# The seams between phases of a two-block transformer kernel, done token block by token block

## The chip, the cores and the metric

One core of a Trainium2 chip runs the whole program. The metric is device time in microseconds, the median of several runs; a profiled execution shows where it goes.

## What is computed

256 tokens of width 2048 go through two transformer blocks, all in float32. What matters here is the chain of matrix products and the norms between them:

```python
# first block (attention left out)
x = x + rmsnorm(mix @ w_out, post_mix_g)
h = rmsnorm(x, pre_ffn_g)
u = causal_dwconv(h @ w_up, conv_w, conv_b)
gate, val = split(u)
y = (gelu(gate) * val) @ w_down          # 5632 -> 2048
x = x + rmsnorm(y, post_ffn_g)
# second block
h = rms_norm(x, norm_attn_w) * (1 + sc_a) + sh_a
q, k, v, u = split(h @ w_in)
x = x + g_a * (concat(attn, pool) @ w_out)
hm = rms_norm(x, norm_mlp_w) * (1 + sc_m) + sh_m
x = x + g_m * (square(relu(hm @ w_up)) @ w_down)   # 2048 -> 8192 -> 2048
return rms_norm(x, final_norm_w)
```

A norm runs along the 2048 columns of a token, so it needs the last column chunk of the product before it, but only for that token.

## The kernel before

The 256 tokens are two blocks of 128 (`b` = 0, 1), one token per partition. Every product goes through column chunks of 512. A chunk is accumulated over the depth in steps of two 128-row tiles: 8 steps for a depth of 2048, 6 in the third down phase ("down1c"). Phases follow one another in the table `PHASES`; those of interest end with down1c and are followed by in2 (seam A), out2 followed by mlp2 (seam B), and the end of mlp2 (the tail, C).

Precision comes from a split of each number into a rounded high part and the rest, so each product is three matmuls: high by high, high by low, low by high. For a step's weights (512 KB) SyncE loads a slot of `raw` (8 slots, `load`, L347), ScalarE writes the high part `w_hi` (`hi`, L573), VectorE the rest `w_lo` (`lo`, L1047), each 128 x 1024, into a ring of 4 slots. `hi(s)` waits for the weights in `raw` and, through `step_done`, for step s-4 to be done; `lo(s)` waits for `hi(s)`; `load` of step s+8 waits for `lo(s)`. TensorE's `step` (L1755) waits for both and runs 12 matmuls, both blocks together, six each. Into PSUM tensor `G` go the products, two banks for an even chunk and two for an odd one; `T` takes transposes.

The activations of a new phase are made from `x`: rows are scaled by the reciprocal norm into `y` (`scale_rows`, block 0 on ScalarE and block 1 on VectorE, or both on VectorE for mlp2), TensorE transposes them (`turn`, L1789, eight units of 256 columns, four transposes of 128 x 128 each), ScalarE applies gain and shift in two 256-wide activations and copies to `h_hi` (`high_shifted`, L559), VectorE subtracts for `h_lo` (`low_shifted`, L1130). Semaphores count the units: `xn_act`, `xn_dve`, `prep_turned`, `prep_hi`, `h_ready`.

Each engine's program is written out by hand and runs strictly in order; a `begin` on each engine (ScalarE, VectorE, TensorE) interleaves the eight units with the first steps. In the last chunk, `last_steps` (L1818) does only the last two steps block by block, so block 0 ends 12 matmuls earlier. Then VectorE sums and weighs it (L1527 on for seam A, L1654 on for B, L1700 on for C), ScalarE squares it, `root` makes one reciprocal norm for both blocks, and only then does `begin` start. In seam A the norm needs two roots: that of y, and that of the new x, got from sums of squares and cross products (`cross`, L1455; L1540 on) before the new x exists. `down_body` (ScalarE L832, VectorE L1459) puts the norm of the context rows (`ctx_squares`, `root("ctx")`, `ctx_scale`) and the squares of finished y chunks between the weight splits of the down1c chunks.

At the end of the kernel the output is scaled and stored in four transfers of 512 KB, two per block, when the norm of both blocks is known.

Of the kernel before, what the change touches and what calls it, by code (L numbers as in the profile page):

```python
# [69 lines left out]
STEPS = 2 * LOADS  # L70
UP0 = {"up1a": 0, "up1b": 8, "up1c": 16, "mlp2": 22}
# [34 lines left out]
def build(nc, a):  # L106
# [83 lines left out]
    dup1 = place("dup1", [P, NB, 2, 2, DH], "x")  # L190
    dup2 = place("dup2", [P, 2 * NB, KV2, 2, DH], "tmp")
# [321 lines left out]
    def _(act):  # L513
# [58 lines left out]

        def hi(s, d=0, width=N):  # L573

            act.wait_ge(raw_full[s % 8], 32 * (s // 8 + 1) + d * 4)
            if s >= 4:
                act.wait_ge(step_done, s - 3 + d)
            act.activation(w_hi[:, s % 4, :, 0:width], raw[:, s % 8, :, 0:width],  # L578
                           ACT.Copy).then_inc(hi_ready, 1)
# [252 lines left out]
        def down_body(s, c):  # L832

            if c == 1:
                his(s + 3, 3)
                y_squares(0)
                his(s + 6, 3)
            elif c == 2:
                act.wait_ge(ctx_in, 16)
                hi(s + 3)  # L840
                ctx_squares(0)
                hi(s + 4)
                ctx_squares(1)
                hi(s + 5)
                y_squares(1)
                hi(s + 6)
                ctx_squares(2)
                hi(s + 7)
                ctx_squares(3)
                hi(s + 8)  # L850
            else:
                hi(s + 3)
                root("ctx")
                hi(s + 4)
# [38 lines left out]
        act.wait_ge(bank_evac, FIRST_EVAC["in2"] - 1)  # L893
        square(y[:, 0, 3 * N:4 * N], sq[:, 0, 3:4])
        act.wait_ge(crossed, 4)
        square(u_buf[:, 0, :], dots[:, 0, 0, 3:4])
        act.wait_ge(bank_evac, FIRST_EVAC["in2"])
        square(y[:, 1, 3 * N:4 * N], sq[:, 1, 3:4])
        act.wait_ge(crossed, 5)
        square(u_buf[:, 1, :], dots[:, 0, 1, 3:4])  # L900
        root("y2")
        root("in2")
        scale = scale_rows(x, y, lambda q: rstdx[:, 0:1])
        act.wait_ge(rstd_ready, STAT["in2"] + 1)

        def in2_scale(q):
            act.wait_ge(x_new, X_NEW["in2"] + q + 1)
            scale(q)

        begin(2 * FIRST_LOAD["in2"], lambda q: high_shifted("in2", q, comb, adac[:, 0, :], h_hi), in2_scale)  # L910


# [71 lines left out]
        for c in range(4):  # L984
            if c == 0:
                his(s0 + 7, 4)
            else:
                if c == 3:
                    sqrt_table()
                body(s0 + 8 * c, n=7 if c == 3 else 8)  # L990
                new_squares("out2")(c - 1)
        for b in range(NB):
            act.wait_ge(x_new, X_NEW["out2"] + 3 + b + 1)
            square(x[:, b, 3 * N:4 * N], sq[:, b, 3:4])
        root("up2")
        begin(2 * FIRST_LOAD["mlp2"], lambda q: high_shifted("up2", q, comb, adac[:, 3, :], h_hi))
# [1256 lines left out]
```

## Time and profile before

| | us |
|---|---|
| median of 3 runs | 2223.4 |
| lowest and highest | 2220.48, 2223.8 |
| profiled execution, its own time | 2221.93 |
| its span, first to last instruction | 2220.2 |
| mean granted TensorE clock | 0.982 |

The page gives busy times by engine, the chain of work that ended last and the costliest groups. Questions to the trace give a timeline (start, duration, engine, line, operation, count, idle time before it and what ended it), groups by line with mean durations, and sums by stretch. PE is TensorE, ACT is ScalarE, DVE is VectorE, SPq is SyncE's DMA queue. A granted clock of 1 is 2.4 GHz, 0.5 is 1.2 GHz. Times in a timeline count from the start of the span.

### The profile page before, as it was taken

The numbers are of one execution on the slowest core, as the hardware profiler recorded it, in microseconds if no ns is written. First come the engines' busy times: TensorE is split into PE (matmuls) and PEld (weight loads), VectorE is DVE, ScalarE is ACT, GpSimd is POOL, SyncE is SP. The second block draws the span as 40 slices with busy tenths as digits, with TensorE's granted clock in tenths as the row PEclk, the third lists the DMA queues.
The fourth block names the chain that finished last, engine by engine and source line by source line (L and its number), as shares of the span: only waits on it lengthen the run. The fifth ranks groups of instructions, "written<-read, shape, count | busy, mean of one in ns | idle before, by whom it ended". The sixth has DMA issues, their size and how long they took to land.

```text
span 2220.2 us, 32332 instructions
## 1 busy us (share of the span) xinstructions
PE 2170.0 (98%) x10240; PEld 1796.3 (81%) x10240; DVE 1509.0 (68%) x1884; ACT 1078.0 (49%) x1449; POOL 133.5 (6%) x233
## 2 busy tenths in 40 slices
PE   8999999999999999999989999999999999999998
PEld 7888887888788888888867778878888887888876
DVE  7996788788896887767675354556545655655656
ACT  6545655555334554355477355454434433433433
POOL 3110001000110000100000000000000000000000
PEclk9999999999999999999989999999999999999999
DMA  9887087888896888978745341547666665766652
GB/s 338 294 261 234 2 301 226 263 278 268 264 300 222 263 276 282 321 221 256 228 133 182 99 158 48 173 159 268 212 194 228 223 195 183 244 191 210 226 173 103
DMA packets 277677, 482.85 MB, mean 217 GB/s; under 512 B 25996, under 2 KB 118484, under 8 KB 276256
## 3 DMA queue, kind: packets, MB, share of 16 engines
q1 hardware_dynamic: 247168, 367.22, 50.5%
q0 software_dynamic: 30192, 113.72, 16.7%
q8 instruction: 83, 1.36, 0.2%
q14 instruction: 58, 0.48, 0.1%
q10 hardware_dynamic: 176, 0.08, 0.0%
HBM read 478.81 MB, written 2.11 MB: 217 GB/s over the span
## 4 chain that ended last, share of the span: by engine, by line
PE 94%; ACT 2%; DVE 2%; issue 1%; DMA 0%; POOL 0%; ACTq 0%; DVEq 0%; POOLq 0%
PE G L1769 28%; PE G L1771 28%; PE G L1770 28%; PE T L2035 1%; PE T L2149 1%; PE T L1842 1%; PE T L1956 1%; PE T L1800 1%; PE G L1936 1%; PE G L2129 1%; ACT w_hi L578 1%; ACT junk L524 0%; PE T L1981 0%; DVE w_lo L1052 0%; PE T L1983 0%
## 5 line engine op out<-in xcount | busy, mean ns | idle before, releaser
L1052 DVE TENSOR_TENSOR w_lo<-raw,w_hi 128x1024 fp32r<-128x1024 f32 x696 | 839.5, 1217 | 462.1 <-ACT w_hi L578 459.7
L578 ACT ACTIVATE w_hi<-raw 128x1024 fp32r<-128x1024 f32 x696 | 732.3, 1055 | 849.8 <-PE G L1771 844.1
L1769 PE MATMUL G<-w_hi,h_hi 128*128 128x512 f32 (+1 forms) x1904 | 749.9, 394 | 7.9 <-issue 4.2
L1771 PE MATMUL G<-w_hi,h_lo 128*128 128x512 f32 (+1 forms) x1904 | 742.1, 390 | 0.0
L1770 PE MATMUL G<-w_lo,h_hi 128*128 128x512 f32 (+1 forms) x1904 | 741.8, 390 | 0.0
L1769 PEld LDWEIGHTS G<-w_hi,h_hi 128*128 128x128 f32 x1904 | 360.1, 189 | 82.5 <-issue 7.8
L1771 PEld LDWEIGHTS G<-w_hi,h_lo 128*128 128x128 f32 x1904 | 359.8, 189 | 74.8
L1770 PEld LDWEIGHTS G<-w_lo,h_hi 128*128 128x128 f32 x1904 | 360.4, 189 | 71.6
L1769 PE MATMUL G<-w_hi,a_hi 128*128 128x512 f32 x880 | 347.4, 395 | 2.2 <-issue 1.1
L1771 PE MATMUL G<-w_hi,a_lo 128*128 128x512 f32 x880 | 345.1, 392 | 0.0
L1770 PE MATMUL G<-w_lo,a_hi 128*128 128x512 f32 x880 | 345.0, 392 | 0.0
L1769 PEld LDWEIGHTS G<-w_hi,a_hi 128*128 128x128 f32 x880 | 167.0, 190 | 39.2 <-issue 3.5
L1770 PEld LDWEIGHTS G<-w_lo,a_hi 128*128 128x128 f32 x880 | 166.9, 190 | 35.0 <-issue 0.5
L1771 PEld LDWEIGHTS G<-w_hi,a_lo 128*128 128x128 f32 x880 | 166.7, 189 | 35.1
L446 POOL DMA_DIRECT2D ada_w<-in_w_ada x192 | 101.9, 531 | 1419.8 <-DVE ada_acc L1070 894.9
L1070 DVE SCALAR_TENSOR_TENSOR ada_acc<-ada_w,silu,ada_acc 128x1024 f32<-128x1024 f32 x122 | 153.7, 1280 | 30.5 <-DMA ada_w<-in_w_ada 30.4
L1070 DVE SCALAR_TENSOR_TENSOR ada_third<-ada_w,silu,ada_third 128x1024 f32<-128x1024 f32 x60 | 76.9, 1282 | 57.8 <-DMA ada_w<-in_w_ada 57.8
L1160 DVE SCALAR_TENSOR_TENSOR ada_acc<-ada_w,silu,ada_acc 128x1024 f32<-128x1024 f32 x64 | 79.2, 1279 | 0.2 <-DMA ada_w<-in_w_ada 0.2
L1417 DVE SCALAR_TENSOR_TENSOR conv<-T,convw,conv 128x255 f32<-128x255 f32 (+1 forms) x176 | 72.6, 475 | 7.0 <-ACT conv L809 4.7
L601 ACT ACTIVATE u_buf<-G,rstdx 128x512 f32<-128x512 f32 x44 | 27.9, 686 | 34.8 <-PE G L1771 34.5
L815 ACT ACTIVATE conv<-conv 128x512 f32<-128x512 f32 x22 | 13.9, 633 | 60.6 <-DVE conv L1417 60.6
L809 ACT ACTIVATE conv<-T,convw 128x256 f32<-128x256 f32 x88 | 42.5, 563 | 0.8
(273 smaller groups left out, 1225.9 us busy)
## 6 DMA issues: line engine op xcount, KB each, us to landing
ada_w<-in_w_ada POOLq DMA_DIRECT2D x192, 512.0 KB, 5.0
raw<-in_w_up SPq DMA_DIRECT2D x352, 256.0 KB, 4.5
raw<-in_w_mlp_up SPq DMA_DIRECT2D x256, 256.0 KB, 2.9
raw<-in_w_mlp_down SPq DMA_DIRECT2D x256, 256.0 KB, 3.4
raw<-in_w_in SPq DMA_DIRECT2D x208, 256.0 KB, 4.0
raw<-in_w_down SPq DMA_DIRECT2D x176, 256.0 KB, 4.8
raw<-in_w_out SPq DMA_DIRECT2D x128, 256.0 KB, 3.8
raw<-in_w_in SPq DMA_DIRECT2D x16, 136.0 KB, 3.5
```

The source lines that it names most:

```text
L446: pool.dma_start(ada_tiles(run)[:, half, :], w_ada[:, bass.ds(t + first // 2, 1), part * D + half * ADA_HALF:part * D + (half + 1) * ADA_HALF]
L578: act.activation(w_hi[:, s % 4, :, 0:width], raw[:, s % 8, :, 0:width], ACT.Copy).then_inc(hi_ready, 1)
L601: act.activation(dst(b), G[:, 2 * parity + b, 0:width], func, scale=scale).then_inc(bank_evac, 1)
L809: ins = act.activation(conv[:, j, :], tt(0)[:, j, :], ACT.Identity, scale=convw[:, 2, bass.ds(t + dt, 1)], bias=convw[:, 3, bass.ds(t + dt ...
L1052: dve.tensor_tensor(w_lo[:, s % 4, :, 0:width], raw[:, s % 8, :, 0:width], w_hi[:, s % 4, :, 0:width].bitcast(F32), ALU.subtract).then_inc ...
L1070: ins = dve.scalar_tensor_tensor(out=acc[:, half, :], in0=ada_tiles(run)[:, half, :], scalar=silu[:, c, bass.ds(dt + (first + k) // 2, 1)] ...
L1160: ins = dve.scalar_tensor_tensor(out=ada_acc[:, c, half, :], in0=ada_w[:, half, :], scalar=silu[:, c, k // 2:k // 2 + 1], in1=ada_acc[:, c ...
L1417: ins = dve.scalar_tensor_tensor(out=conv[:, j, k:TOK], in0=tt(0)[:, j, 0:TOK - k], scalar=convw[:, tap, bass.ds(t + dt, 1)], in1=conv[:, ...
L1769: pe.matmul(out, ah, wh, start=f, stop=False)
L1770: pe.matmul(out, ah, wl, start=False, stop=False)
L1771: mm = pe.matmul(out, al, wh, start=False, stop=l)
L1800: mm = pe.transpose(bank(q)[:, TOK * j + b * P:TOK * j + b * P + P], src[:, b, (2 * q + j) * P:(2 * q + j + 1) * P], ident)
```

## The change

- The last chunk of down1c, out2 and mlp2 runs all its steps for block 0 and then all for block 1 (`last_chunk`). For that, all its weights must stand at once, so SBUF regions that are free then take some steps' halves (`SLOT`, `halves`): two at seam A, four at B, four in the tail. `hi` waits for the last user of its own slot (`BEFORE`).
- Each norm at these places is made per block: roots `y2_0`, `in2_0`, `y2_1`, `in2_1`, `up2_0`, `up2_1`, `final_0`, `final_1`.
- Activations of in2 and mlp2 are made in eight parts of one block and 512 columns (`PARTS`), in place of units of both blocks and 256 columns. `high_part` uses four 128-wide activations and one copy; `in2_scale` is 512 wide. At seam A ScalarE scales the parts of block 0, at seam B VectorE scales all.
- The first chunk of in2 and mlp2 runs steps 0 to 5 for block 0, then for block 1, then steps 6 and 7 for both (`first_chunk`); transposes of the parts stand between. The first two parts (A) or three (B) are turned inside the last chunk's block-1 pass.
- In down1c the context norm moves one chunk earlier in `down_body`. ScalarE's chunk 1 is now `his(s+3, 3)`, `y_squares(0)`, then `hi` of s+6, s+7, s+8 with `ctx_squares(0)` and `(1)` between; its chunk 2 is `hi(s+3)`, `ctx_squares(2)`, `hi(s+4)`, `ctx_squares(3)`, `hi(s+5)`, `y_squares(1)`, `root("ctx")`, `hi(s+6)`, four `ctx_scale`, `hi(s+7)`, four `ctx_scale`, `hi(s+8)`; its chunk 3 is `his(s+3, 3)`, `y_squares(2)`. VectorE's root, scaling and cross products follow suit. `cross` of the last chunk writes its unused product to PSUM.
- At the end each block is normed, scaled and stored by itself.

The diff, cut to its core; first the tables and ScalarE:

```diff
+IN2, OUT2, UP2 = (2 * FIRST_LOAD[n] for n in ("in2", "out2", "mlp2"))
+SLOT = {s: s % 4 for s in range(STEPS)}
+SLOT |= {IN2 - 6 + k: ("in2", k) for k in range(2)} | {IN2 + 4 + k: ("in2", k) for k in range(2)}
+SLOT |= {UP2 - 8 + k: ("act", k) for k in range(4)} | {UP2 + 4 + k: ("act", k) for k in range(2)}
+SLOT |= {STEPS - 8 + k: ("h", k) for k in range(4)}
+PARTS = ((0, 0), (0, 1), (0, 2), (1, 0), (1, 1), (1, 2), (0, 3), (1, 3))
...
+        def high_part(name, u, gain, shift):
+            act.wait_ge(prep_turned, PREP[name] + u + 1)
+            if u >= 2:
+                act.wait_ge(h_ready, PREP[name] + u - 1)
+            for j in range(4):
+                k = 4 * PARTS[u][1] + j
+                ins = act.activation(split_part(u)[:, j, :], bank(u)[:, P * j:P * j + P], ACT.Identity,
+                                     scale=gain[:, k:k + 1], bias=shift[:, k:k + 1])
+            ins.then_inc(tmp_act, 1)
+            act.wait_ge(tmp_act, SHIFTED[name] + u + 1)
+            act.activation(part_of(h_hi, u), split_part(u), ACT.Copy).then_inc(prep_hi, 1)
...
-            if s >= 4:
-                act.wait_ge(step_done, s - 3 + d)
+            if BEFORE[s] is not None:
+                act.wait_ge(step_done, BEFORE[s] + 1 + d)
...
+        y2_squares(0)
+        root("y2_0", 0, 1)
+        hi(IN2)
+        root("in2_0", 0, 1)
+        act.wait_ge(rstd_ready, STAT["in2_0"] + 1)
+        in2_scale(0)
+        in2_scale(1)
+        in2_high(0)
+        hi(IN2 + 1)
+        in2_scale(2)
+        y2_squares(1)
+        in2_high(1)
+        hi(IN2 + 2)
+        root("y2_1", 1, 1)
+        in2_high(2)
+        root("in2_1", 1, 1)
+        his(IN2 + 3, 2)
+        in2_high(3)
+        hi(IN2 + 5)
+        in2_scale(6)
+        in2_high(4)
+        in2_high(5)
+        in2_high(6)
+        hi(IN2 + 6)
+        in2_high(7)
+        hi(IN2 + 7)
...
+        x_square("out2", 0)
+        root("up2_0", 0, 1)
+        up2_high(0)
+        hi(UP2)
+        up2_high(1)
+        hi(UP2 + 1)
+        up2_high(2)
+        hi(UP2 + 2)
+        x_square("out2", 1)
+        root("up2_1", 1, 1)
+        hi(UP2 + 3)
+        hi(UP2 + 4)
+        up2_high(3)
+        hi(UP2 + 5)
+        up2_high(4)
```

On VectorE, again for seam A and then for seam B:

```diff
+        y2_sum(0)
+        y2_cross(0)
+        y2_root(0)
+        in2_root(0)
+        in2_rows(0)
+        lo(IN2)
+        in2_rows(1)
+        in2_low(0)
+        lo(IN2 + 1)
+        in2_rows(2)
+        y2_sum(1)
+        in2_low(1)
+        lo(IN2 + 2)
+        y2_cross(1)
+        y2_root(1, lambda: in2_low(2))
+        in2_root(1, lambda: lo(IN2 + 3))
+        in2_rows(3)
+        lo(IN2 + 4)
+        in2_rows(4)
+        in2_low(3)
+        lo(IN2 + 5)
...
+        x_sum(0)
+        root("up2_0", rstdx[:, 0:1], blocks=slice(0, 1))
+        scale_part(0)
+        scale_part(1)
+        scale_part(2)
+        up2_low(0)
+        lo(UP2)
+        up2_low(1)
+        lo(UP2 + 1)
+        up2_low(2)
+        lo(UP2 + 2)
+        x_sum(1)
+        root("up2_1", rstdx[:, 1:2], at=1, blocks=slice(1, 2), meanwhile=lambda: lo(UP2 + 3))
+        scale_part(3)
+        scale_part(4)
+        lo(UP2 + 4)
+        scale_part(5)
+        up2_low(3)
+        lo(UP2 + 5)
```

On TensorE:

```diff
+        def last_chunk(s, n, acts, e, ready, between=lambda k: None):
+            pe.wait_ge(bank_evac, e)
+            block_steps(s, range(n), 0, 1, acts, n - 1, ready)
+            block_steps(s, range(n), 1, 1, acts, n - 1, None, between)
...
+        def first_chunk(name, s, turned):
+            def part(b):
+                return lambda k: (h_ready, PREP[name] + PARTS.index((b, k // 2)) + 1)
+            def blocks(b, ks, *parts):
+                block_steps(s, ks, b, 0, H[0], 7, part(b))
+                for u in parts:
+                    turn_part(name, u)
+            blocks(0, (0, 1), *((2,) if turned < 3 else ()))
+            blocks(0, (2, 3))
+            blocks(0, (4,), 3)
+            blocks(0, (5,), 4, 5)
+            blocks(1, (0, 1), 6)
+            blocks(1, (2, 3), 7)
+            blocks(1, (4, 5))
+            steps(s, 6, 8, 0, H, lambda k: (h_ready, PREP[name] + UNITS))
```

`block_steps` runs six matmuls per step for one block, waits for `hi` and `lo` of a step in the block-0 pass only, and counts `step_done` in the block-1 pass only. On VectorE `y2_sum` adds the chunk's product to y and weighs it, `y2_cross` makes the cross product, `in2_rows` updates x for one part (and scales it, for block 1), `in2_low` subtracts for `h_lo`; `x_sum` is the like for seam B.

## Rows read from the trace of the kernel before

**Rows 1.** Page, busy time of each engine; and shares of the chain that ended last:
```profile
PE 2170.0 (98%) x10240; PEld 1796.3 (81%) x10240; DVE 1509.0 (68%) x1884; ACT 1078.0 (49%) x1449; POOL 133.5 (6%) x233
...
PE 94%; ACT 2%; DVE 2%; issue 1%; DMA 0%; POOL 0%; ACTq 0%; DVEq 0%; POOLq 0%
```

**Rows 2.** Stretches table: busy time, clock, DMA share, GB/s:
```profile
1147.50:1187.80 40.30, 29.89 (x130) 24.05 (x130) 32.24 (x60) 28.12 (x51) 0.00 (x0) 0.83 0.37 117
1473.80:1508.10 34.30, 29.66 (x129) 24.42 (x129) 24.87 (x40) 22.36 (x36) 6.12 (x6) 0.85 0.50 173
2209.40:2220.20 10.80, 0.00 (x0) 0.00 (x0) 4.24 (x10) 3.48 (x7) 0.00 (x0) 0.71 0.49 194
```

**Rows 3.** Timeline, TensorE, seam A: start, us, line, operation, count, idle before:
```profile
1147.20 0.39 PE L1833 MATMUL G<-w_hi,a_lo 128*128 128x512 f32 x1
1156.83 2.19 PE L1800 MATMUL T<-consts,y 128*128 128x128 f32 x8 [9.24 <-ACT y L545]
...
1160.85 0.78 PE L1769 MATMUL G<-w_hi,h_hi 128*128 128x512 f32 x1
...
1187.52 0.39 PE L1771 MATMUL G<-w_hi,h_lo 128*128 128x512 f32 x1
```

**Rows 4.** Timeline, TensorE, seam B:
```profile
1473.60 0.39 PE L1833 MATMUL G<-w_hi,h_lo 128*128 128x512 f32 x1
1477.73 2.82 PE L1800 MATMUL T<-consts,y 128*128 128x128 f32 x12 [3.75 <-DVE y L1113]
...
1507.25 0.39 PE L1771 MATMUL G<-w_hi,h_lo 128*128 128x512 f32 x1
...
1507.93 0.39 PE L1771 MATMUL G<-w_hi,h_lo 128*128 128x512 f32 x1
```

**Rows 5.** Timeline, TensorE, two other idle pieces:
```profile
367.38 2.82 PE L1800 MATMUL T<-consts,x 128*128 128x128 f32 x12 [2.83 <-DVE x L1363]
...
401.73 1.09 PE L2035 MATMUL T<-consts,u_buf 128*128 128x128 f32 x8 [1.36 <-ACT u_buf L601]
```

**Rows 6.** Groups by form, ScalarE: line, shapes, count, busy us, mean ns:
```profile
L578 ACT ACTIVATE w_hi<-raw 128x1024 fp32r<-128x1024 f32 x688 | 727.1, 1060 | 843.0 <-PE G L1771 837.3 <-DMA raw<-in_w_in 5.1
...
L567 ACT ACTIVATE conv<-T,adac,comb 128x256 f32<-128x256 f32 x32 | 16.1, 554 | 6.0 <-PE T L1800 5.9
...
L700 ACT ACTIVATE sm<-sm,nm 128x128 f32<-128x128 f32 x32 | 12.6, 394 | 24.0 <-DVE nm L1285 23.8
...
L692 ACT ACTIVATE vx<-p 128x128 f32<-128x128 f32 x2 | 0.5, 296 | 0.0
```

**Rows 7.** Timeline, ScalarE, seam A:
```profile
1149.16 0.63 ACT L524 ACTIVATE junk<-y 128x512 f32<-128x512 f32 x1 [2.64 <-DVE y L1532]
1149.69 0.18 ACT L524 ACTIVATION_READ_ACCUMULATOR junk<-y 128x1 f32 x1
...
1159.01 0.63 ACT L571 ACTIVATE h_hi<-conv 128x512 fp32r<-128x512 f32 x1
```

**Rows 8.** Groups by form, VectorE:
```profile
L1052 DVE TENSOR_TENSOR w_lo<-raw,w_hi 128x1024 fp32r<-128x1024 f32 x688 | 833.9, 1223 | 458.3 <-ACT w_hi L578 456.1 <-DVE ones_again L1092 0.2
L1070 DVE SCALAR_TENSOR_TENSOR ada_acc<-ada_w,silu,ada_acc 128x1024 f32<-128x1024 f32 x122 | 153.7, 1280 | 30.5 <-DMA ada_w<-in_w_ada 30.4
...
L1363 DVE SCALAR_TENSOR_TENSOR x<-y,rstd,x 128x256 f32<-128x256 f32 x28 | 12.1, 480 | 0.1
```

**Rows 9.** Timeline, VectorE, around seam B and at the end:
```profile
1454.73 1.22 DVE L1052 TENSOR_TENSOR w_lo<-raw,w_hi 128x1024 fp32r<-128x1024 f32 x1
...
2192.61 3.49 DVE L1052 TENSOR_TENSOR w_lo<-raw,w_hi 128x1024 fp32r<-128x1024 f32 x3
...
2209.39 0.69 DVE L1336 TENSOR_TENSOR y<-G,row 128x512 f32<-128x512 f32 x1 [0.50 <-PE G L1833]
...
2212.23 0.17 DVE L1105 RECIPROCAL rstdx<-ssq 128x2 f32<-128x2 f32 x1 [0.27 <-ACT ssq L535]
```

**Rows 10.** DMA query, 2212 to 2221 us: GB/s in 40 slices:
```profile
GB/s 0 0 0 0 0 0 0 0 0 309 419 419 419 400 364 419 437 400 400 382 401 437 400 364 419 419 383 437 364 437 437 364 91 0 0 0 0 0 0 0
```

More of the change, by code:

```diff
@@ L891, in _, with y2_squares, in2_scale, in2_high @@
                     body(s0 + per * c, n=per)
[L893 to L910, printed above, removed]
+        def y2_squares(b):
+            act.wait_ge(bank_evac, FIRST_EVAC["in2"] - 1 + b)
+            square(y[:, b, 3 * N:4 * N], sq[:, b, 3:4])
+            act.wait_ge(crossed, 4 + b)
+            square(u_buf[:, b, :], dots[:, 0, b, 3:4])
+        def in2_scale(u):
+            cols = slice(PARTS[u][1] * N, PARTS[u][1] * N + N)
+            act.wait_ge(x_new, X_NEW["in2"] + u + 1)
+            act.activation(y[:, 0, cols], x[:, 0, cols], ACT.Copy, scale=rstdx[:, 0:1]).then_inc(xn_act, 1)
+        def in2_high(u):
+            high_part("in2", u, comb, adac[:, 0, :])
+        y2_squares(0)
[24 more added lines that the diff above has]
+        hi(IN2 + 7)
         s0 = 2 * FIRST_LOAD["in2"]
@@ L1026, in _ @@
         for b in range(NB):
-            act.wait_ge(x_new, X_NEW["final"] + 3 + b + 1)
-            square(x[:, b, 3 * N:4 * N], sq[:, b, 3:4])
-        root("final")
-        act.wait_ge(rstd_ready, STAT["final"] + 1)
-        for b in range(NB):
+            x_square("final", b)
+            root(f"final_{b}", b, 1)
+            act.wait_ge(rstd_ready, STAT[f"final_{b}"] + 1)
             for c in (1, 3):
@@ L1525, in _, with y2_sum @@
                     ada_finish(fin_down)
-        for b in range(NB):
+        def y2_sum(b):
             if b == 0:
@@ L1558, in _ @@
+        lo(IN2 + 5)
+        in2_rows(5)
+        in2_rows(6)
+        in2_low(4)
+        in2_low(5)
+        in2_rows(7)
+        in2_low(6)
+        lo(IN2 + 6)
+        in2_low(7)
+        lo(IN2 + 7)
         cos = tab2[:, COS2:COS2 + 2 * DH].rearrange("p (b d) -> p b d", b=NB)
@@ L1837, in last_steps, with block_steps @@
                     mm.then_inc(block_done, 1)
+        def block_steps(s, ks, b, parity, acts, last, ready=None, between=lambda k: None):
+            hi, lo = acts
+            for k in ks:
+                if b == 0:
+                    pe.wait_ge(hi_ready, s + k + 1)
+                    pe.wait_ge(lo_ready, s + k + 1)
+                if ready is not None:
+                    pe.wait_ge(*ready(k))
+                whole, rest = halves(s + k)
+                for j in range(STEPK):
+                    ah, al = (t[:, STEPK * k + j, b * P:b * P + P] for t in (hi, lo))
+                    out = G[:, 2 * parity + b, :]
+                    pe.matmul(out, ah, whole[:, j, :], start=k == 0 and j == 0, stop=False)
+                    pe.matmul(out, ah, rest[:, j, :], start=False, stop=False)
+                    mm = pe.matmul(out, al, whole[:, j, :], start=False, stop=k == last and j == STEPK - 1)
+                if b == 1:
+                    mm.then_inc(step_done, 1)
+                elif k == last:
+                    mm.then_inc(block_done, 1)
+                between(k)
```

270 lines of the change are left out of this document (168 added, 102 removed).

## The prediction

> **What bounds the kernel now.** I read the page first: TensorE is busy 98% of the span and holds 94% of the chain that ended last [rows 1]. So only what makes TensorE's stream denser can shorten the kernel, and what delays it lengthens the kernel one for one. The stretches table shows the places of the edit [rows 2]. At the full clock a 512-wide matmul follows the one before by 0.227 us (three in 0.68) [rows 4], and four transposes take 0.43 (eight need 1.09, less the last one's own delay) [rows 5]. A first chunk is 96 matmuls and eight groups of four transposes, 21.8 + 3.4 = 25.2 us. Seam A (down1c to in2) takes 40.3, so 15.1 are lost: 9.24 idle in one piece while the norm is made [rows 3], and the rest to the clock, whose mean is 0.83, which makes 0.34 x 40.3 = 13.7 us at 1.2 GHz. Seam B (out2 to mlp2) takes 34.3 and loses 9.1, 3.75 of it one gap, mean clock 0.85 [rows 2, 4]. The tail C is 10.8 us behind the last matmul. The change can win at most about 15 + 9 + a few.
>
> **How I cost it.** All new orders are written out by hand, so I laid them on a timetable: an instruction starts when its engine is free and its last input has landed, plus 0.04 to 0.06 us. Laid over the old order from the last matmul of each phase, this ends seam A at 1187.9 and seam B at 1508.1; the trace has 1187.75 and 1508.16 [rows 3, 4], so the method is good to a few tenths. Prices: `hi` 1.06, `lo` 1.22, of which 0.08 to 0.1 overlaps the next instruction [rows 6, 8]; a square with its accumulator read 0.72 and an `h_hi` copy of 512 columns 0.63 [rows 7]; a two-tensor VectorE op over 512 columns 0.69, tiny ones 0.17 to 0.2 [rows 9]; a three-operand op over 512 columns 0.75, between 0.48 for 256 and 1.28 for 1024 [rows 8].
>
> **One new price.** `high_part` does a part as four 128-wide activations in place of two of 256. The 256-wide one takes 0.55, that is 1.02 for a unit's two [rows 6]. No row has it 128 wide: below it stand a plain 128-wide copy, 0.30, and a 128-wide exponential with a pointer bias, 0.39; above it the 256-wide 0.55 [rows 6]. I take 0.45 and 1.56 for four with overlap, ends 1.2 and 1.95. With the copy a part costs ScalarE 2.1 where a unit cost 1.55: eight parts make 4.4 us more on ScalarE per seam. (The Trainium skill, "ScalarE: Activation LUTs", section "What ACT_TABLE_LOAD costs", gives a fixed cost per activation, more with each pointer operand, and about 0.09 us of overlap; by its figures four would cost an estimated 1.64. The trace agrees at 256 columns.)
>
> **Seam A, the last chunk.** It must start at 1147.4 - 6 x 2.72 = 1131.1. Its block-0 pass wants a step's weights every 1.36 us. Context squares, root and scaling are moved into chunk 2, ahead of `hi(IN2-6)` to `hi(IN2-4)` on both engines, and the eviction of chunk 2 stands before `lo(IN2-3)`. My timetable has `lo(-4)` ready at 1134.6 and `lo(-3)` at 1136.9: TensorE waits 0.75 and 1.0. Block 0 ends at 1141.2 and block 1 would end at 1149.2. DVE is free at 1141.8 (chunk 2's cross products are queued ahead), the sum, norm and second root give the reciprocal for block 0 at 1146.7, `hi(IN2)` having slipped in between. Scaled columns come at 1148.2 and 1150.1, transposes of part 0 at 1148.8. So far this is as meant.
>
> **Seam A, the first chunk.** Here the new order ties the engines into a serial chain. Part 0 is split at 1153.0 (TensorE idle 2.5). `lo(IN2+1)` is ready at 1154.4, and only behind it and `in2_rows(2)` does VectorE take block 1's sum (1155.1). ScalarE has `y2_squares(1)` queued ahead of `in2_high(1)`, so part 1, whose transposes were done at 1150.7, waits until 1157.3, is low at 1160.3, and `lo(IN2+2)`, queued behind it, comes at 1161.8: TensorE idle 5.5. Then cross, root, `high(2)`, the second root, and only then `hi(IN2+3)`; `lo(IN2+3)` lands at 1169.6: idle 6.5. `lo(IN2+4)` at 1172.1: idle 1.2. Part 3's transposes stand on TensorE behind step 4; its split precedes `hi(IN2+5)`, `lo(IN2+5)` at 1178.6: idle 4.7. The last parts are ScalarE's 2.1 each, back to back, and the last `h_ready` comes at 1191.4. The chunk ends at 1196.9 at the full clock, 9.2 later than before. The order gives `hi` and `lo` of steps 2, 3 and 5 the place behind work that waits for block 1 or for TensorE; in the old order both engines kept running.
>
> **Seam B** by the same walk: the last chunk runs unbroken (eight weights in four spare slots; the old eviction of chunk 2 ended before 1454.9, `lo(UP2-5)` just in time), the norm of block 0 ends at 1466.3 and parts 0 to 2 are turned inside block 1's pass. The old gap of 3.75 goes, and the first chunk starts at 1475.2 rather than 1481.4. But `x_sum(1)` stands behind `lo(UP2+2)`, and square and root ahead of `hi(UP2+3)`: waits of 1.7, 3.7, 0.8 and 4.7 for `lo` of steps 2 to 5. End 1511.3, 3.2 later than before.
>
> **The tail C.** Before the last chunk VectorE evicts chunk 2 and gates it; its next `lo` start at 2192.6 [rows 9]. The chunk starts at 2187.4, its fourth step in single-block time at 2191.5, and needs the first of these, ready at 2193.9: 2.4 us lost. Behind the last matmul the chain of sum, square, root is as long as it was, 3.0 (2209.4 to 2212.4) [rows 9], but two of four output transfers have gone. The four ran 5.3 us at about 410 GB/s [rows 10], so two are worth 2.6, less the second's wait for its issue. Net -0.3, between -2.9 (no stall) and +1.
>
> **The clock.** After 3.75 us of idleness the transposes ran slow, twelve in 2.82 [rows 4], also after 2.83 [rows 5]; after 1.36 eight took 1.09 [rows 5]. The new gaps of 5.5, 6.5 and 4.7 in A and 3.7 and 4.7 in B are of the first kind. At 1.2 GHz from about 1160 to 1185 in A, the matmuls on the chain (three short bursts and transposes) double: A ends 3.4 later, +12.6, or +11 if it recovers in between; B gets +5 to +7. (The Trainium skill, "TensorE: Matmul & The Clock Gate", section "HAM oscillation — how this bites in real kernels", says that gaps in the matmul stream drop the clock again and again; rows agree for single gaps, none shows a run of them.)
>
> **Sum.** A +11, B +5.5, C -0.3: +16, on the profiled run's own 2221.9 (span 2220.2) 2238; it stands 1.5 under the median of 2223.4, on which the forecast is 2239.5. What follows either seam stays bound by TensorE and moves with it.
>
> **Rivals.** (1) Same order, clock stays at 2.4 GHz in most of it: A +9.2, B +3.2, C -0.3 = +12, 2235.5. For it: its pieces of work are short. Chance 0.25. (2) The clock stays low to the end of both first chunks and the block-0 passes starve more, because both engines must bring a step in 1.36 us where `lo` alone takes 1.14: A +15, B +8, C +1 = +24, 2247. Chance 0.13. The change would then not do what it says, finish block 0 early. (3) Faster: the norm of block 1 is in fact hidden. It decides at part 1: were its low half ready by the end of step 1 of block 0, 1155.8 (mine is 1160.3), and `lo` of steps 2 to 5 not late either, TensorE would idle in A only 1.75 + 0.5 + 2.5, keep its clock and lose 4.7 in place of 15.1; B would lose about 2 in place of 9.1; with C -0.3 that is -18, 2206. (The Trainium skill, "Perfetto Trace Analysis", section "Optimizing Scalar/DVE Operations", says that breaking up instructions can let work finish sooner where ScalarE or VectorE cause bubbles; by that rule it is this case.) Against it: the squares stand ahead of `in2_high(1)` in a queue that runs in order. Chance 0.08. (4) The stalls of A are half of mine and B comes out even or better: within 4 us. Chance 0.05.
>
> **Chances.** Forecast (A +10 to +13, B +4 to +7) 0.49, rivals 0.25, 0.13, 0.08, 0.05. About 0.2%, 4.4 us, is what a measurement here can tell. Slower 0.87, same 0.05, faster 0.08. The range takes in the low end of (1), with cheap 128-wide activations (A another 2 less) and no stall in C, 2228, and (2) in part: 2228 to 2249.
>
> **What would show it.** In A the profile after should show TensorE idle in four or five pieces of 2 to 7 us between 1150 and 1185, released by VectorE's `w_lo` and `h_lo`, a first chunk ending near 1197 to 1200, and ScalarE's squares of block 1 ahead of part 1's activations. In B matmuls start about 6 us earlier, yet the chunk ends later. In C TensorE waits once for `w_lo`. It would be wrong if the waits for `w_lo` of steps 2, 3 and 5 are short, or if part 1's activations run before block 1's squares.

## The result

The changed kernel takes 2239.5 us (median of 5 runs, 2230.7 to 2243.8) beside 2223.4 for the kernel before on the same chip (5 runs, 2214.5 to 2227.7): a ratio of 1.007, interval 1.0047 to 1.0092. Measured again, beside experiment 4, it gave 1.0083 (1.0058 to 1.0108). The sign and the size were as forecast; that the median met 2239.5 to a tenth is luck, since the interval is 10 us wide. The profiled execution is the shortest of the five; its own time is 2230.7, its span 2229.0. The page of after, which answers to [rows 1]:

```profile
span 2229.0 us, 32345 instructions
...
PE 2167.0 (97%) x10240; PEld 1790.1 (80%) x10240; DVE 1506.8 (68%) x1876; ACT 1084.0 (49%) x1481; POOL 133.0 (6%) x233
...
PE 94%; ACT 3%; issue 1%; DVE 1%; DMA 0%; POOL 0%; ACTq 0%; DVEq 0%; POOLq 0%
```

The page says little: TensorE still holds 94% of the chain. The stretches say more. Each runs from the start of the last chunk of a phase to the end of the next phase's first chunk (the third to the end of the span). Columns: stretch, length, busy time (count) by engine, granted clock, DMA share, GB/s. First the kernel before, which shows the whole seams where [rows 2] shows only their second parts, then after:

```profile
core 0 of [0], span 2220.2 us
...
1131.11:1187.75 56.64, 46.23 (x201) 37.33 (x200) 44.71 (x83) 40.62 (x75) 0.00 (x0) 0.88 0.43 135
1452.07:1508.16 56.09, 51.45 (x226) 42.27 (x224) 37.52 (x54) 33.20 (x51) 6.12 (x6) 0.91 0.55 181
2187.43:2220.20 32.77, 21.92 (x97) 17.83 (x95) 19.51 (x25) 10.85 (x18) 0.00 (x0) 0.90 0.16 65
```

```profile
core 0 of [0], span 2229.0 us
...
1126.00:1192.64 66.64, 47.91 (x202) 37.02 (x200) 43.22 (x71) 41.34 (x82) 0.00 (x0) 0.90 0.36 114
1456.94:1519.84 62.90, 53.40 (x226) 42.77 (x225) 32.86 (x46) 31.69 (x62) 5.04 (x4) 0.89 0.43 138
2196.35:2229.00 32.65, 22.21 (x97) 17.75 (x95) 19.87 (x28) 7.03 (x15) 0.00 (x0) 0.94 0.16 65
```

A is 10.0 longer, B 6.8, the tail 0.1 shorter: +16.7, where the forecast had +11, +5.5, -0.3, which makes +16.2. In the second trace of the same kernel (beside experiment 4) A is 66.9 and B 63.0 long. Where the 10 us of A are is seen in TensorE's waits. These rows answer to [rows 3]; the single wait of 9.24 is gone. In its place (start, duration, line, operation, count, idle before):

```profile
1129.51 0.47 PE L2036 MATMUL G<-w_hi,a_hi 128*128 128x512 f32 x1 [0.62 <-ACT w_hi L626]
...
1131.84 0.47 PE L2036 MATMUL G<-w_hi,a_hi 128*128 128x512 f32 x1 [0.72 <-issue]
...
1148.18 0.47 PE L2036 MATMUL G<-w_hi,h_hi 128*128 128x512 f32 x1 [2.29 <-ACT w_hi L626]
...
1156.76 0.61 PE L2036 MATMUL G<-w_hi,h_hi 128*128 128x512 f32 x1 [5.13 <-DVE w_lo L1147]
...
1164.23 0.77 PE L2036 MATMUL G<-w_hi,h_hi 128*128 128x512 f32 x1 [4.73 <-ACT in_hi L626]
...
1173.55 0.47 PE L2036 MATMUL G<-in_hi,h_hi 128*128 128x512 f32 x1 [4.51 <-issue]
```

The first two are the starved block-0 pass of down1c's last chunk, the next four stand before steps 0, 2, 3 and 5 of block 0. The names of the releasers mislead here. TensorE waits for `hi_ready`, `lo_ready` and `h_ready` together. At 1164.23 the page names ScalarE's `in_hi`, but VectorE's low half of step 3 ended at that moment: its row starts at 1162.91 and lasts 1.23. At 1173.55, "issue", a low half starts at 1172.22 and lasts 1.23. Why VectorE was late with them:

```profile
1157.36 0.16 DVE L1196 TENSOR_REDUCE ssq<-sq 128x1 f32<-128x4 f32 x1
1157.56 0.15 DVE L1197 TENSOR_SCALAR ssq<-ssq 128x1 f32<-128x1 f32 x1
1160.04 0.69 DVE L1229 TENSOR_TENSOR h_lo<-conv,h_hi 128x512 fp32r<-128x512 f32 x1 [2.33 <-ACT h_hi L619]
...
1162.91 1.23 DVE L1147 TENSOR_TENSOR w_lo<-raw,w_hi 128x1024 fp32r<-128x1024 f32 x1 [1.22 <-ACT w_hi L626]
```

VectorE is not busy, it stands in its own queue: idle 2.33 for part 2's high half, then 1.22 for `hi(IN2+3)`, which stands on ScalarE behind two roots and a part. Seam B shows the same kind of wait, 1.38, 3.27 and 4.51 before steps 2, 3 and 5, where [rows 4] had one of 3.75. The tail has the forecast stall:

```profile
2202.85 0.47 PE L2036 MATMUL G<-spare_hi,a_hi 128*128 128x512 f32 x1 [2.26 <-issue]
```

The profiled after is 8.8 longer in span, not 16.7, so it won 7.9 elsewhere: 5.1 ahead of A (which starts at 1126.0 here and at 1131.1 in before), nothing between A and B, 2.8 between B and the tail. Experiments 1 and 8 below take that up.

### The profile page after: what moved, and what is told of

Read it like the earlier page. It is cut to its first block, busy times and chain, and to the rows that moved or that the text cites. A ratio compares the mean times of both kernels' runs of the same rounds, so it can differ in the third digit from the quotient of the medians.

```text
span 2229.0 us, 32345 instructions
## 1 busy us (share of the span) xinstructions
PE 2167.0 (97%) x10240; PEld 1790.1 (80%) x10240; DVE 1506.8 (68%) x1876; ACT 1084.0 (49%) x1481; POOL 133.0 (6%) x233
## 3 DMA queue, kind: packets, MB, share of 16 engines
q1 hardware_dynamic: 247168, 367.22, 50.2%
q0 software_dynamic: 30192, 113.72, 16.7%
## 4 chain that ended last, share of the span: by engine, by line
PE 94%; ACT 3%; issue 1%; DVE 1%; DMA 0%; POOL 0%; ACTq 0%; DVEq 0%; POOLq 0%
PE G L1953 27%; PE G L1955 27%; PE G L1954 27%; PE T L2281 1%; PE T L2395 1%; PE G L2036 1%; PE T L2202 1%; PE G L2038 1%; PE G L2037 1%; PE T L2088 1%; ACT conv L615 1%; PE G L2182 1%; PE G L2375 1%; ACT w_hi L626 1%; PE T L1984 0%
## 5 line engine op out<-in xcount | busy, mean ns | idle before, releaser
L626 ACT ACTIVATE w_hi<-raw 128x1024 fp32r<-128x1024 f32 x682 | 716.5, 1055 | 813.5 <-PE G L1955 806.9
L1147 DVE TENSOR_TENSOR w_lo<-raw,w_hi 128x1024 fp32r<-128x1024 f32 x682 | 821.7, 1216 | 429.5 <-ACT w_hi L626 427.2
L1953 PE MATMUL G<-w_hi,h_hi 128*128 128x512 f32 (+1 forms) x1832 | 718.1, 392 | 6.2 <-issue 2.6
L1955 PE MATMUL G<-w_hi,h_lo 128*128 128x512 f32 (+1 forms) x1832 | 711.4, 388 | 0.0
L1954 PE MATMUL G<-w_lo,h_hi 128*128 128x512 f32 (+1 forms) x1832 | 710.9, 388 | 0.0
L1953 PEld LDWEIGHTS G<-w_hi,h_hi 128*128 128x128 f32 x1832 | 344.9, 188 | 78.0 <-issue 6.8
L1954 PEld LDWEIGHTS G<-w_lo,h_hi 128*128 128x128 f32 x1832 | 345.0, 188 | 68.5
L1953 PE MATMUL G<-w_hi,a_hi 128*128 128x512 f32 x840 | 331.2, 394 | 2.5 <-issue 1.7
L1954 PE MATMUL G<-w_lo,a_hi 128*128 128x512 f32 x840 | 329.0, 392 | 0.0
L1955 PE MATMUL G<-w_hi,a_lo 128*128 128x512 f32 x840 | 329.0, 392 | 0.0
```

Source lines behind the costliest of these rows:

```text
L626: act.activation(halves(s)[0][:, :, 0:width], raw[:, s % 8, :, 0:width], ACT.Copy).then_inc(hi_ready, 1)
L1147: dve.tensor_tensor(rest[:, :, 0:width], raw[:, s % 8, :, 0:width], whole[:, :, 0:width].bitcast(F32), ALU.subtract).then_inc(lo_ready, 1)
L1953: pe.matmul(out, ah, wh, start=f, stop=False)
L1954: pe.matmul(out, ah, wl, start=False, stop=False)
L1955: mm = pe.matmul(out, al, wh, start=False, stop=l)
```

## The experiments

My theory: the order of ScalarE's and VectorE's queues in the two first chunks makes a serial chain, and that is the loss. The rivals: TensorE's half clock; the extra ScalarE work of 128-wide activations; a loss that isn't in the seams at all. Lengths of A and B are always measured as above (56.6 and 56.1 in before, 66.6 and 62.9 in after).

**1. One part of the change at a time.** Three kernels, each the kernel before with one place changed.

```diff
 # A alone (PE; ScalarE's and VectorE's parts of the same seam go with it)
-        begin("in2", y, s0, 0, r)
-        steps(s0, 3, 8, 0, H, r)
+        first_chunk("in2", s0, 2)
 # B alone
-        begin("up2", y, s0, 0, r)
-        group2(s0, e0, u0, begun=3)
+        first_chunk("up2", s0, 3)
+        group2(s0, e0, u0, begun=8)
 # C alone
+                if last and c == 3:
+                    last_chunk(s + 56, 8, A[0], e + 12, ready)
```

> Of the change only seam A (down1c to in2) is made: context work moved into chunk 2, block-first last chunk, norm per block, first chunk by blocks. Seam B and the tail are those of before. Theory (the order of the two queues makes a serial chain in the first chunk): the trace of after has A 10.0 us longer than before, so 2223.4 + 10 = 2233.4, ratio 1.0045. Rival (the parts share the loss through the clock, what is won or lost elsewhere): if the 8 us that the profiled run won outside the seams belonged to the change, A alone would give about +5 or less, ratio under 1.0025.

> Of the change only seam B (out2 to mlp2) is made. Theory: the trace of after has B 6.8 us longer, so 2230.2, ratio 1.003; at the full clock my timetable gives +3.2, 1.0014, so a value between the two says how much the half clock adds. Rival (B is about even and the whole loss is A's): ratio 1.000.

> Of the change only the tail is made (last chunk by blocks in four spare slots, root per block, two of four output transfers early). Theory: 2.3 us of waiting for one low half and 2.6 us less of output transfer cancel: -0.1 to -0.3 us, ratio 0.9999. Rival (the stall costs more than the transfers give, or the other way round): off by over 2 us, ratio under 0.999 or over 1.001.

A alone: 1.0046 (1.0027 to 1.0064), its seam 66.9 long. B alone: 1.0027 (1.0011 to 1.0042), its seam 63.2. C alone: 0.9996 (0.9979 to 1.0013), with the same stall of 2.26. 1.0046 and 1.0027 are 10.2 and 6.0 us, and the seams are 10.3 and 7.1 longer than before's. So the loss lies in A and B, about 3 to 2, and the tail is even, as the walk (the prediction's timetable) had it.

**2. One swap at the point that the prediction named.** The prediction let its rival (3) decide at part 1, where ScalarE has block 1's squares ahead of `in2_high(1)`.

```diff
-        y2_squares(1)
         in2_high(1)
+        y2_squares(1)
         hi(IN2 + 2)
```

> The kernel after with one edit: on ScalarE in2_high(1) stands ahead of y2_squares(1), so that part 1 is split before block 1's squares. My prediction named this place as the point from which the other sign decides. Rival (that place alone makes the wait): the 5.1 us wait before step 2 of block 0 goes down by the two squares and more, about 3 us, and the time to about 3 us under after, ratio 1.0055 or less. Theory (both queues are tied together, so that one swap is not enough): VectorE has block 1's sum ahead of part 1's low half and the low half of step 2 behind it, and hi(IN2+2) still stands behind the squares; my timetable moves the wait by 0.1 us: ratio that of after, 1.007, and the wait before step 2 at 5.0 us.

Ratio 1.0076 (1.0052 to 1.01). The wait before step 2:

```profile
1159.76 0.77 PE L2036 MATMUL G<-w_hi,h_hi 128*128 128x512 f32 x1 [5.01 <-DVE w_lo L1147]
```

5.01 in place of 5.13: the timetable's 0.1, and nothing won. Part 1 was split 1.5 us earlier, but the squares now stood before `hi(IN2+2)`, so the low half of step 2 came no sooner. I had named the place rightly and its weight wrongly: it is one link of two that are late together. The other links were not swapped one by one.

**3. The order of both queues, nothing else edited.** With the same timetable I laid an order of both engines, same instructions, in which as far as possible hi and lo of the coming steps are never behind work that waits for block 1. Seam A's two queues, shortened and side by side (in seam B `hi` and `lo` of steps 1 to 5 move forward in the same way):

```diff
 # ScalarE, seam A                       # VectorE, seam A
-in2_scale(0); in2_scale(1)             -in2_rows(0); lo(IN2); in2_rows(1)
-in2_high(0); hi(IN2+1)                 -in2_low(0); lo(IN2+1); in2_rows(2)
-in2_scale(2); y2_squares(1)            -y2_sum(1); in2_low(1); lo(IN2+2)
-in2_high(1); hi(IN2+2); root y2_1      -y2_cross(1); y2_root(1, in2_low(2))
-in2_high(2); root in2_1                -in2_root(1, lo(IN2+3))
-his(IN2+3, 2); in2_high(3); hi(IN2+5)  -in2_rows(3); lo(IN2+4); ...
+hi(IN2+1); in2_scale(0); hi(IN2+2)     +in2_rows(0); in2_rows(1); in2_rows(2)
+in2_high(0); in2_scale(1)              +lo(IN2); y2_sum(1); lo(IN2+1)
+y2_squares(1); hi(IN2+3); root y2_1    +y2_cross(1); y2_root(1, in2_low(0))
+in2_high(1); in2_scale(2); hi(IN2+4)   +lo(IN2+2)
+root in2_1; in2_high(2); hi(IN2+5)     +in2_root(1, in2_low(1), lo(IN2+3))
+in2_high(3)                            +lo(IN2+4); in2_low(2); in2_rows(3); ...
```

> The kernel after with ScalarE's and VectorE's queues of seam A's first chunk put in another order and nothing else changed (same instructions): hi/lo of steps 1 to 5 ahead of block 1's squares, roots and parts, block 1's sum ahead of the low halves of parts 0 and 1. Theory (the loss in A is the order): on my timetable the first chunk ends 15 us earlier (1182.2 on before's clock, where after has 1197.1 and before 1187.9), no wait over 2.5 us is left, the long ones being the start (2.3) and transposes of part 1 (1.9). So 15 under after: about 1.000 of before, with B and C as in after, at most 0.3% either way for the clock. Rival (the half clock or the extra work of 128-wide activations is the loss): the order changes little, under 4 us, ratio 1.005 or more.

> The kernel after with the two queues of seam B's first chunk in another order: hi/lo(UP2) to UP2+5 ahead of block 1's norm and parts as far as they can stand there. Theory: the first chunk ends 9.3 us earlier on the full-clock timetable (1502.1; after 1511.4, before 1508.1), 12 with the clock that after lost there; waits of 0.6, 0.5, 1.0 and 0.5 are left. Ratio 1.007 - 0.005 = 1.002. Rival (clock or activations): under 3 us, 1.0055 or more.

A in the new order: ratio 1.0008 (0.9991 to 1.0025), seam 52.8 against a forecast of 51.6. B in the new order: 1.0012 (0.9992 to 1.0032), seam 50.2. Their stretches (seam A of the first kernel, then seam B of the second):

```profile
1128.66:1181.48 52.82, 45.85 (x201) 35.39 (x200) 42.86 (x71) 40.89 (x83) 0.00 (x0) 0.97 0.46 145
```

```profile
1459.71:1509.91 50.20, 48.67 (x226) 38.90 (x225) 32.05 (x46) 31.46 (x62) 5.04 (x4) 1.00 0.51 173
```

TensorE's waits in seam A of the first:

```profile
1149.80 0.44 PE L2063 MATMUL T<-consts,y 128*128 128x128 f32 x2 [1.64 <-ACT y L950]
...
1152.66 0.47 PE L2036 MATMUL G<-w_hi,h_hi 128*128 128x512 f32 x1 [2.21 <-DVE h_lo L1230]
...
1160.77 0.47 PE L2036 MATMUL G<-in_hi,h_hi 128*128 128x512 f32 x1 [0.33 <-DVE h_lo L1230]
...
1175.92 0.47 PE L1953 MATMUL G<-w_hi,h_hi 128*128 128x512 f32 x1 [0.53 <-DVE h_lo L1230]
```

The same instructions take 13.8 us less in A and 12.7 less in B, and both seams are now under those of before. This decides against the activations as the bound: their work is as it was, only the queues were edited. The clock did not stay as it was. With the waits gone it rose from 0.90 and 0.89 to 0.97 and 1.00. Experiment 6 gives after the same 0.97 and 1.00 with its old queues, and its seams are 65.5 and 59.0 long. So at equal clock the order is worth 12.7 us in A and 8.8 in B, and the clock, which follows the order, the rest.

**4. VectorE's order alone.** The right column above without the left one.

> The kernel after with VectorE's new order of e5 in seam A and ScalarE's old one. Theory (the two queues are tied together, neither order alone brings the 14 us of both): my timetable ends the first chunk 5.3 us earlier than after's, with waits of TensorE before steps 0, 2, 3, 4, 5 of block 0 of 4.7, 2.0, 1.6, 0.6, 4.7 and 1.5 before step 6: 1.007 - 0.0024 = 1.0046. Rival (VectorE's queue was the one that held everything, ScalarE's is only carried along): nearly all of e5's gain, ratio 1.001 to 1.002.

Ratio 1.0054 (1.0032 to 1.0076), seam A 63.5: 3.1 less than after, of the 13.8 that both orders bring. That is the theory's side: VectorE's queue alone does not bring the gain. ScalarE's new order alone was not run. The size in the seam was missed, 3.1 for 5.3 (the ratio allows either), and the trace shows how:

```profile
1158.42 0.47 PE L2035 MATMUL G<-w_hi,h_hi 128*128 128x512 f32 x1 [4.45 <-DVE h_lo L1229]
...
1168.03 0.47 PE L2035 MATMUL G<-w_hi,h_hi 128*128 128x512 f32 x1 [3.03 <-ACT in_hi L626]
...
1177.72 0.77 PE L2035 MATMUL G<-in_hi,h_hi 128*128 128x512 f32 x1 [4.51 <-issue]
```

The waits of 4.7 and 4.7 are there. The 2.0 and 1.6 before steps 2 and 3 have become one of 3.03, because behind the wait of 4.45 TensorE ran nine matmuls 0.43 us apart, half clock, and part 2's transposes stand behind them.

**5. Less ScalarE work.** One 512-wide activation per part, 0.77 us, in place of four that take 1.49. It leaves out the scale and shift of three column groups in four, so its result is another one. It takes away 0.72 a part, about 1.5 times the 0.49 that the finer cut had added (two 256-wide ones took 1.00 in before), not three times as the expectation has it.

```diff
-            for j in range(4):
-                k = 4 * PARTS[u][1] + j
-                ins = act.activation(split_part(u)[:, j, :], bank(u)[:, P * j:P * j + P], ACT.Identity, ...)
+            k = 4 * PARTS[u][1]
+            ins = act.activation(conv[...], bank(u), ACT.Identity, ...)   # 512 wide
```

> The kernel after, but a part is scaled and shifted by one 512-wide activation with the first column group's scale and shift in place of four 128-wide ones with their own (so three quarters of the modulated activations get another column's scale and shift). It takes about 0.9 us of ScalarE away from each of 16 parts, 14 us in all, three times what the finer cut had added. Rival (the extra ScalarE work is the loss): both seams fall under before's, ratio under 1.000. Theory (order): on the timetable A ends 5.3 and B 4.7 earlier than in after with all four long waits still there, each 1 us shorter: A 4.6, 5.5, 1.2, 3.8; ratio 1.007 - 0.0045 = 1.0025.

Ratio 1.0041 (1.0024 to 1.0058), over 1.000: as the whole cause the rival falls. The waits in A are 4.40, 3.85 and 3.78 where after has 5.13, 4.73 and 4.51. Taking more work away than the change had added still left the long waits, each about 0.8 shorter. The timetable was off in the parts: A gained 1.3 (forecast 5.3), B 5.8 (4.7). In B that is most of the 6.8 that after loses: its seam is 57.1 long here, 1.0 over before's, at a clock of 0.97. So in B the run does not clear ScalarE's work: with less of it most of the loss goes, while the new order of experiment 3 wins twice as much. Seam A:

```profile
core 0 of [0], span 2230.1 us
...
1134.21:1199.51 65.30, 50.01 (x202) 38.87 (x201) 43.22 (x71) 35.86 (x59) 0.00 (x0) 0.84 0.37 118
```

A's mean clock is 0.84 where after has 0.90 (0.87 in its second trace): 0.16 x 2 x 65.3 = 21 us at half clock against 13 (17). TensorE's idle time in A fell by 3.4 us, from 18.7 to 15.3, and part of it was given back in slow matmuls: 22 follow one another at half pace in place of 15, which costs 1.4 us. The rest of what was given back, 0.7, I can't place.

**6. TensorE kept busy in its waits.** Matmuls whose result is overwritten, shorter than the waits (the unused output of the cross product moves to another bank for them).

```diff
-            cross(3, b, u_buf[:, b, :], G[:, 1, :])
+            cross(3, b, u_buf[:, b, :], G[:, 2 * b + 1, :])
...
+            def fill(k, n):
+                whole = halves(s + k)[0]
+                for _ in range(n):
+                    pe.matmul(G[:, 1, :], h_hi[:, 0, 0:P], whole[:, 0, :], start=True, stop=True)
             def blocks(b, ks, *parts):
-                block_steps(s, ks, b, 0, H[0], 7, part(b))
+                for k in ks:
+                    if b == 0:
+                        fill(k - 1, {"in2": {2: 18, 3: 17, 5: 16}, "up2": {2: 3, 3: 11, 5: 16}}[name].get(k, 0))
+                    block_steps(s, (k,), b, 0, H[0], 7, part(b))
```

> The kernel after with TensorE kept busy in its long waits: ahead of steps 2, 3 and 5 of block 0 in both first chunks stand 18, 17 and 16 (A) and 3, 11 and 16 (B) matmuls of 512 columns into the bank that block 1 has not begun; their results are overwritten. They are shorter than the waits at the full clock (0.227 us each), so they cost nothing if it holds. Rival (the half clock makes much of the loss): A falls to the full-clock timetable or under, by 1 us at least, B from +6.8 to +3.2, and both together to ratio 1.005 or less. Theory (in A the queues are the bound and the half clock falls mostly into waits; in B it counts): A gains about 1, B 3 to 3.6, ratio 1.005; granted clock near 1 in both chunks, and the waits that are left 1.0, 0.9, 0.9 (A) and 0.7, 1.2, 1.1 (B). If the ratio stays at 1.007 or above with the clock at 1, the half clock had no part in the loss.

Ratio 1.0032 (1.0016 to 1.0048). The stretches of seams A and B:

```profile
core 0 of [0], span 2229.6 us
...
1133.90:1199.39 65.49, 57.33 (x253) 44.68 (x251) 43.25 (x71) 41.25 (x83) 0.00 (x0) 0.97 0.37 117
1463.70:1522.74 59.04, 55.67 (x256) 44.30 (x255) 32.60 (x46) 31.59 (x62) 5.05 (x4) 1.00 0.44 147
```

A is 1.15 shorter than in after, B 3.9, about as expected; the clock is 0.97 and 1.00. The rival had written down the same bounds, so this run does not choose between the two; it measures the clock's part. In B that part is more than half of the 6.8 lost. One caution: B with the same instructions was 62.9 to 63.2 long in five traces and 61.0 in one, that of experiment 3's first kernel, so the 3.9 is good to about 2. So the half clock costs after about 5 us in its seams, little of it in A, where the queues are late whatever TensorE's speed. That is 5.0 of the 8 to 11 us (the two ratios of after less this one's) by which this kernel is under after. The ratio was forecast as 1.005, above the interval measured; for the rest see 8.

**7. The same for the kernel before.** 36 and 14 such matmuls ahead of `turns` in `begin`, at seams A and B.

```diff
+            n = {"in2": 36, "up2": 14}.get(name, 0)
...
+            for _ in range(n):
+                pe.matmul(G[:, 0, :], w_hi[:, s % 4, 1, 0:P], w_hi[:, s % 4, 0, :], start=True, stop=True)
             turns(name, src, 0, 3)
```

> The kernel before with TensorE kept busy in its own long wait of each seam: 36 (A) and 14 (B) matmuls of 512 columns into a bank that the first chunk overwrites, right behind the last chunk, 8.2 and 3.2 us of the waits of 9.24 and 3.75. Theory (before pays for the half clock in its seams as after does, so that the order alone is worth more than the plain difference of the two): with a full clock my timetable ends A at 1186.7 in place of 1187.9 and B at 1505.0 in place of 1508.1, 4.3 us together, ratio 0.998. Rival (before's half clock falls wholly beside waits and costs nothing): 1.000, seams of 56.6 and 56.1 us as before.

Ratio 0.9963 (0.9948 to 0.9977): 8.2 us, twice what was expected.

```profile
core 0 of [0], span 2207.8 us
...
1128.54:1184.84 56.30, 53.37 (x237) 43.41 (x236) 44.73 (x83) 40.50 (x75) 0.00 (x0) 0.94 0.43 137
1449.16:1502.25 53.09, 50.97 (x240) 41.90 (x239) 37.52 (x54) 33.20 (x51) 6.11 (x6) 1.00 0.59 192
```

The seams give 0.3 and 3.0 of it, where 1.2 and 3.1 were expected: in A the clock reached only 0.94, ten matmuls still ran at half pace. Before pays for the half clock too, 3.3 against after's 5.0. With both filled, A differs by 9.2 and B by 5.9: the price of the change at a nearly full clock. The 8.2 is more than the seams show; see 8.

**8. Where the rest of those 8 us is.** The traces of the runs above tell it. In before, TensorE's longest wait outside the seams (the kernel's first microseconds left out) stands where its loop over the groups of mlp2 jumps back for the second turn. In before, in after, in the filled after (6) and in the filled before (7):

```profile
1845.92 0.80 PE L1769 MATMUL G<-w_hi,h_hi 128*128 128x512 f32 x1 [3.93 <-issue]
```

```profile
1856.94 0.80 PE L1953 MATMUL G<-w_hi,h_hi 128*128 128x512 f32 x1 [2.09 <-issue]
```

```profile
1856.86 0.47 PE L1953 MATMUL G<-w_hi,h_hi 128*128 128x512 f32 x1 [0.31 <-issue]
```

```profile
1836.50 0.47 PE L1769 MATMUL G<-w_hi,h_hi 128*128 128x512 f32 x1 [0.42 <-issue]
```

Behind the 3.93 the clock is halved for 6.8 us, behind the 2.09 for 3.4 here (behind the waits of 2.1 to 2.6 in experiment 3's two kernels and in 9's hardly at all), behind the last two never. From the first transposes of mlp2's `u_buf` to the last matmul of the kernel, less the tail's stall of 2.3 where there is one, before takes 695.4 us, the filled before 688.9, after 692.9 and 692.8 in its two traces, the filled after 690.6. The eight traces of kernels with after's TensorE program lie between 691.1 and 692.9 but for one, the swap of experiment 2 with 696.6; their mean is 692.7. So the filled before wins 3.3 in its seams and 6.4 here, 9.7 (measured 5 to 12). The wait goes with the program, if not exactly: 3.9 and 4.2 in before and with C alone, 2.3 and 3.1 with A or B alone (the latter put down to `w_lo`), 1.8 to 3.2 in the eight traces, 0.3 and 0.4 in the two with some 50 more matmuls ahead of the loop. What sets these programs apart for TensorE is the code ahead of the jump; that its amount decides is my reading, no run varied it alone. (The Trainium skill, "Runtime: NRT & Kernel Launch", section "Instruction fetch mechanics", says that a taken branch whose target isn't at hand must have the target's page fetched before it goes on. The rows agree in kind: it is an "issue" wait at a jump. Why its length differs, no run here shows.)

So about 3 of the 7.9 us that the profiled after won outside its seams come with the change, and 16.7 - 3 = 14 is what it costs in all, beside 15.6 by the medians' ratio. The rest of the 7.9, the 5.1 ahead of A, is scatter: from the start to one mark in down1c the same after took 1109.5 us in one trace and 1116.0 in another, with stretches at half clock in different number. The moved context work costs nothing there: the three chunks ahead of A's stretch and the transposes between them take 57.5 us in before and in both traces of after.

**9. All that was learned, in one kernel.** Both new orders, and in the tail VectorE's gating of chunk 2 behind the last chunk's low halves.

```diff
                     down_evac(c, s + 32 + 8 * c + 8, d)
-                    dve.wait_ge(bank_evac, ...)
-                    gated(c)
-                    weighed_out(cols, slice(0, NB))
+                    if c < 2:
+                        gate(c)          # the three lines above
                 else:
+                    gate(2)
                     gated(c)
```

> The kernel after with both new orders of e5 and e6, and in the tail VectorE's gating of chunk 2 behind the low halves of the last chunk instead of ahead of them. Theory: A 15 us and B 9.3 to 12 under after, the tail 2.3: 26 to 29 under after, 2211 against 2223.4 of before, ratio 0.9945 (between 0.992 and 0.997): faster than both. Rival (clock or activations): 1.003 or more.

2208.5 us, ratio 0.9938 (0.9913 to 0.9962): faster than before by 14 us and than after by about 30.

```profile
core 0 of [0], span 2204.9 us
...
1132.45:1185.26 52.81, 45.84 (x201) 35.40 (x200) 42.85 (x71) 40.87 (x82) 0.00 (x0) 0.97 0.44 144
1449.59:1499.77 50.18, 48.62 (x226) 38.92 (x225) 32.36 (x46) 31.46 (x62) 5.04 (x4) 1.00 0.50 173
2174.77:2204.90 30.13, 21.92 (x97) 17.83 (x95) 19.76 (x28) 7.03 (x15) 0.00 (x0) 0.94 0.18 70
```

VectorE's and ScalarE's busy times are those of after within 0.5 us in A and B; only idle time and slow matmuls went. Two things are not settled. No kernel was run in which before's own instructions are put in a better order. And before with its waits filled (7) stands at 0.9963: its interval overlaps with this one's. In the traces this kernel's seams are 3.5 and 2.9 us shorter than that one's and its stretch of mlp2 (8) is 2.2 longer, so of the 14 us much is the clock and the jump, which matmuls that nobody reads also win back.

## Why the prediction was right, point by point

- **What bounds it**: right. TensorE's waits in the seams, and the slow matmuls behind them, are the difference, give or take the loop's jump. That the total met so closely is in part luck: A was 1.0 below its term, B 1.3 above, and the 3 us of the jump were not in the sum.
- **The last chunk of A**: the forecast waits of 0.75 and 1.0 measured 0.62 and 0.72; block 0's reciprocal and part 0 came on time (step 0 could start 22.2 us into the stretch; the walk had 21.9).
- **The first chunk of A**: waits of 2.5, 5.5, 6.5, 1.2, 4.7 forecast; 2.29, 5.13, 4.73, none, 4.51 measured. The sum of the third and fourth is off by 3.0. TensorE's bursts between the waits ran at half clock, so part of what I had as waiting was spent in slow matmuls. The end was +9.2 by the walk, +11 with the clock, and is +10.0.
- **Price of four 128-wide activations**: 1.49 against the 1.56 taken (L615).

```profile
1152.31 1.49 ACT L615 ACTIVATE conv<-T,adac,comb 128x128 f32<-128x128 f32 x4
```

- **Seam B**: forecast +5.5, measured +6.8 (+6.8 to +7.1 in five traces, +4.9 in one). The waits were right (1.7, 3.7, 0.8, 4.7 against 1.38, 3.27, none, 4.51).
- **The clock**: the walks at the full clock hold. The filled after is 8.9 (A) and 2.9 (B) over before, the walks had 9.2 and 3.2, so rival (1)'s 12 us is what after would cost if the clock stayed up; it doesn't. What was mis-sized is the share of each seam: I took 1.8 for A and 2.3 for B, measured are 1.15 and 3.9 (give or take 2 in B).
- **The tail**: -0.3 forecast, -0.1 measured. The stall is 2.26 for 2.4; without it (experiment 9) the tail is 2.6 shorter than before's. That is the output transfers' share: from the last matmul to the end it is 8.6 us where before has 11.2, and the sum, square and root take 3.0 in both.
- **"What follows either seam moves with it"**: this step failed, by about 3 us, at the jump of TensorE's loop. The profile of before shows the wait there, 3.93 at 1845.92, and I did not ask what the new TensorE program would do to it. Why it is shorter in after stays open (8). It hid in the scatter of the medians (10 to 20 us by the interval).
- **The low end of the range**: the two reliefs that are named take rival (1) from 2235.5 to 2231 (2 and 2.4 less), not to 2228; nothing in the prediction gives the other 3. It didn't matter here.
- **Rival (3)** had the right mechanism behind it: most of the norm of block 1 can be hidden, and the block-wise form then stands 14 us under before. But its decision point was too narrow: neither the swap at that point (2) nor VectorE's order alone (4) reaches it, both queues together do. (The Trainium skill, "Perfetto Trace Analysis", section "Optimizing Scalar/DVE Operations", says that breaking up instructions may let work complete sooner. In after it did not, in experiment 9 it did, with the same pieces.)

## What to carry to other kernels

When work is cut finer so that a part can start early, the queues of the helper engines must be ordered anew: in an in-order queue every piece that waits for the later part must stand behind what the earlier part's next steps need. Lay both queues on one timetable, since moving one piece on one engine may win nothing (0.1 us of a wait here, 13.8 us of the seam for both orders whole). Compare a walk only with a walk at the same clock, and look at the waits at loop jumps whenever the code ahead of them changes. Before crediting a better order, try what filling the waits alone would win (8.2 us here).

## What the runs showed of the hardware

- A wait of TensorE of "issue" kind at a loop's jump back: 0.3 to 4.2 us, different from one TensorE program to the next and up to 1.4 us apart within one, and up to 6.8 us at half clock behind it.
- Keeping TensorE busy in a wait pays even in the kernel before: B's first chunk is 3.0 us shorter with 14 matmuls whose result nobody reads. After waits of 4.4 to 5.1 us in A the next bursts ran at 1.2 GHz but for their first matmuls, and shortening a wait that stays (5.13 to 4.40) did not prevent it.
- Where an instruction waits for several semaphores, the releaser named can be wrong: seven of the eight waits over 1 us in after's seams and tail ended 0.1 us behind a low half on VectorE (of weights or of activations), and the profile names ScalarE or "issue" for them.
